# Two-layer block on one core: the second norm's sum taken from products of residual and update, and the next two weight units worked tile by tile

## The reference, cut to what matters

```python
h = _modulate(_rms_norm(x, g_pre_mix), sh1, sc1)
y = mixers(h @ w_in) @ w_out
x = x + g1 * _rms_norm(y, g_post_mix)
h = _modulate(_rms_norm(x, g_pre_ffn), sh2, sc2)
f = square(relu(h @ w_ff1)) @ w_ff2
x = x + g2 * _rms_norm(f, g_post_ffn)
```

## Time and profile before

| | |
|---|---|
| median of 3 runs | 1632.98 us (1628.01 to 1635.12) |
| the profiled execution | 1626.87 us, span 1624.9 us |
| PE busy | 1511.0 us, 93% |
| DVE busy | 969.8 us, 60% |
| ACT busy | 913.2 us, 56% |
| chain that ended last | PE 74%, DVE 13%, ACT 10% |
| PE's granted clock, mean | 0.97 of full speed |

### The profile page before, as it was taken

How to read it: one execution, slowest core, us unless ns; L and a number is a source line. 1 busy time by engine, 2 the same in 40 slices (tenths; PEclk the granted TensorE clock), 3 DMA queues, 4 the chain that set the end, 5 groups by cost and what they waited for, 6 DMA issues and landing times.

```text
span 1624.9 us, 25430 instructions
## 1 busy us (share of the span) xinstructions
PE 1511.0 (93%) x10123; PEld 1271.8 (78%) x10123; DVE 969.8 (60%) x1565; ACT 913.2 (56%) x1510; POOL 34.2 (2%) x74
## 2 busy tenths in 40 slices
PE   5999999989999999979988899998999999888887
PEld 3688456658888888838846799998999998887787
DVE  2464578473443434475768766667675766577555
ACT  5654676463232423465666654567786767477745
POOL 3000000000000000000000000000000000001100
PEclk9999999989999999999999999999999999999899
DMA  7731446333433233343316566564544444253232
GB/s 246 241 90 66 156 154 207 127 110 101 133 104 104 78 104 104 112 130 104 104 64 221 185 205 202 188 198 151 177 156 152 150 141 156 79 168 112 85 105 78
DMA packets 223638, 225.37 MB, mean 139 GB/s; under 512 B 8234, under 2 KB 222064, under 8 KB 223472
## 3 DMA queue, kind: packets, MB, share of 16 engines
q1 hardware_dynamic: 222816, 223.63, 42.8%
q0 software_dynamic: 704, 0.12, 0.0%
HBM read 222.68 MB, written 1.05 MB: 138 GB/s over the span
## 4 chain that ended last, share of the span: by engine, by line
PE 74%; DVE 13%; ACT 10%; issue 2%; DMA 1%; SPq 0%; POOL 0%; DVEq 0%; ACTq 0%; POOLq 0%
PE bank L1057 21%; PE bank L1059 21%; PE bank L1058 21%; ACT SH L1739 2%; PE bank L1105 2%; DVE wlo L2169 1%; ACT whi L1602 1%; PE bank L1265 1%; PE bank L1426 1%; DVE AP L2745 1%; PE bank L1454 1%; PE bank L1381 1%; ACT AP L2023 1%; DVE XT L2489 1%; DVE XN L2488 1%
## 5 line engine op out<-in xcount | busy, mean ns | idle before, releaser
L2169 DVE TENSOR_TENSOR wlo<-raw,whi 128x1024 fp32r<-128x1024 f32 (+2 forms) x322 | 387.8, 1208 | 254.1 <-ACT whi L1602 249.3
L1602 ACT ACTIVATE whi<-raw 128x1024 fp32r<-128x1024 f32 (+2 forms) x322 | 335.9, 1046 | 272.7 <-PE bank L1059 254.0
L1057 PE MATMUL bank<-HH,whi 128*128 128x512 f32 (+2 forms) x640 | 245.3, 383 | 18.7 <-DVE HL L2191 15.7
L1058 PE MATMUL bank<-HL,whi 128*128 128x512 f32 (+2 forms) x640 | 241.5, 377 | 0.0
L1059 PE MATMUL bank<-HH,wlo 128*128 128x512 f32 (+2 forms) x640 | 241.4, 377 | 0.0
L1057 PE MATMUL bank<-HA,whi 128*128 128x256 f32 x576 | 165.4, 287 | 13.6 <-DVE LA L2191 5.2
L1058 PE MATMUL bank<-LA,whi 128*128 128x256 f32 x576 | 162.5, 282 | 0.0
L1059 PE MATMUL bank<-HA,wlo 128*128 128x256 f32 x576 | 162.3, 282 | 0.0
L1057 PEld LDWEIGHTS bank<-HH,whi 128*128 128x128 f32 (+1 forms) x640 | 121.2, 189 | 47.4 <-issue 16.0
L1059 PEld LDWEIGHTS bank<-HH,wlo 128*128 128x128 f32 (+1 forms) x640 | 121.2, 189 | 22.9 <-issue 0.5
L1058 PEld LDWEIGHTS bank<-HL,whi 128*128 128x128 f32 (+1 forms) x640 | 121.4, 190 | 22.3 <-issue 0.9
(11 more groups left out here) (377 smaller groups left out, 3072.8 us busy)
## 6 DMA issues: line engine op xcount, KB each, us to landing
raw<-in_w_ff_dram SPq DMA_DIRECT2D x64, 1024.0 KB, 5.4
raw<-in_w_mod_dram SPq DMA_DIRECT2D x48, 1024.0 KB, 5.2
raw<-in_a_w_in_dram SPq DMA_DIRECT2D x40, 1024.0 KB, 5.1
raw<-in_w_in_dram SPq DMA_DIRECT2D x18, 1024.0 KB, 5.3
raw<-in_b_w_in_dram SPq DMA_DIRECT2D x9, 1024.0 KB, 5.3
raw<-in_w_out_dram SPq DMA_DIRECT2D x8, 1024.0 KB, 6.3
raw<-in_ple_w_gate_dram SPq DMA_DIRECT2D x8, 1024.0 KB, 5.2
raw<-in_a_w_out_dram SPq DMA_DIRECT2D x4, 1024.0 KB, 5.1
```

Source lines behind the costliest of these rows:

```text
L1057: nc.tensor.matmul(o, wh, xh, start=start, stop=False, skip_group_check=shared)
L1058: nc.tensor.matmul(o, wh, xl, start=False, stop=False, skip_group_check=shared)
L1602: f(whi[h % HALF_SLOTS][:, 0:n], raw[u.id % RAW_SLOTS][:, (h % 2) * n:(h % 2) * n + n], ACT.Copy)\
L2169: v.tensor_tensor(wlo[h % HALF_SLOTS][:, 0:n], raw[u.id % RAW_SLOTS][:, (h % 2) * n:(h % 2) * n + n], whi[h % HALF_SLOTS][:, 0:n].bitcast( ...
```

## The change

In the product phase ahead of a gap DVE keeps three running sums: `ACC` of y² as before, `ACCC` of (g·y)² and `ACCB` of x·g·y (with `PB` as scratch), where g is the gate with the norm's gain. Behind the last product PE sums them over the partitions by token, in columns (128x1 results, four per sum for 512 tokens), so that root, refinement and the polynomial for the new x² (`post_sums`) run on 128x4; PE spreads both factors over a bank each (`widen`, banks 3 and 4). `norm` then updates x and norms it in one pass. The sum of x² is carried on in `AC`, which `first_sum` fills once. ACT now makes `HH` and `H` of every tile. The two next units are worked tile by tile together, only two of the mods stay ahead of their end, and the third stands behind it.

```diff
     def gap_units(first, second):
-        u0 = without_step(*first)
-        made = [lone_mod(*fill.pop(0), 3 + n) for n in range(3)]
-        u1 = without_step(*second)
-        if len(fill) > 0:
-            made.append(lone_mod(*fill.pop(0), 6))
-        u0.halves, u1.halves = (3, 4), (3, 4)
+        u0, u1 = without_step(*first), without_step(*second)
+        made = [lone_mod(*fill.pop(0), bank) for bank in (5, 7, None)]
+        made[0].pick, made[1].pick = 3, 4
+        for u in (u0, u1):
+            u.halves, u.first_half_done = (3, 4), None
+        if not u0.packed:
+            u0.banks_from = 5
         return u0, u1, made
...
+    def gap_post(l, which, u1, made):
         steps.append(("post", l, which))
+        steps.append(("post_sums", l, which, u1))
+        steps.append(("mod_mm", made[0]))
+
+    def gap_norm(l, which, u0, u1, made):
+        gap_second[l, which] = u1
+        steps.append(("norm_sum", l, which))
+        steps.append(("mod_row", made[0]))
+        steps.append(("mod_mm", made[1]))
         steps.append(("norm", l, which, (0, KC)))
+        for k in range(KC):
+            steps.append(("one_k", u0, k))
+            steps.append(("one_k", u1, k))
+        steps.append(("mod_mm", made[2]))
+        steps.append(("mod_row", made[1]))
+        steps.append(("mod_row", made[2]))
+        steps.append(("unit", u0))
+        steps.append(("unit", u1))
+        for kind in ("mod_pick", "mod_col"):
+            for u in made:
+                steps.append((kind, u))
+        filler(1, (LAYERS, 0))
...
+        def widen(b, src, t):
+            for n, c in enumerate(chunks_of(t)):
+                ins = nc.tensor.matmul(b[:, n * P:(n + 1) * P], bc(src[:, c:c + 1], [P, P]), ident, start=True, stop=True)
+            return ins
...
+        def add_yy(l, which, m):
...
+                    ins = v.scalar_tensor_tensor(out=ACCC[:, ts_], in0=SQ[m % 2][:, ts_], scalar=fG2[:, m, 1 - s:2 - s], in1=ACCC[:, ts_],
+                                                 op0=ALU.mult, op1=ALU.add)
...
+        def add_xy(l, which, m, n=1):
...
+            ins = v.scalar_tensor_tensor(out=x, in0=y, scalar=8.0 / D, in1=x_old, op0=ALU.mult, op1=ALU.mult)
...
+                ins = v.tensor_tensor(acc, acc, x, ALU.add)
...
+        def post_sums(l, which):
...
+            chain(v.tensor_tensor(tmp, columns(banks[4], t, 4), r, ALU.mult))
+            chain(v.tensor_tensor(tmp, tmp, columns(banks[4], t, 0), ALU.add))
+            chain(v.tensor_tensor(tmp, tmp, r, ALU.mult))
+            v.tensor_tensor(acc, acc, tmp, ALU.add).then_inc(*s_poly.tick(("n",) + norm_after[l, which]))
...
+                if before is not None:
+                    dve.wait_ge(s_yg, s_yg.at(before + (b_ - 1,)))
+                    dve.wait_ge(s_wide, s_wide.at(("p",) + before))
+                    chain(v.tensor_tensor(x, YM[:, a_:b_, sl], bc(banks[3][:, 0:n_t].unsqueeze(1), wide_), ALU.mult))
+                    v.tensor_tensor(XT[:, a_:b_, sl], XT[:, a_:b_, sl], x, ALU.add)\
+                        .then_inc(*s_x_new.tick(*(before + (k,) for k in range(a_, b_))))
...
+                v.tensor_tensor(x, XT[:, a_:b_, sl], bc(root.unsqueeze(1), wide_), ALU.mult)\
```

More of the change, by code:

```diff
@@ L185, in build @@
     s_aa = signal("aa")
+    s_products = signal("products")
+    s_poly = signal("poly")
+    s_wide = signal("wide")
     s_ab = signal("ab")
@@ L531, in lone_mod, with w_in_units @@
         u = without_step(mod_units, l, m, m + 1)
[L532 removed]
+        u.alone, u.bank, u.pick = True, bank, bank
         return u
[L535 removed]
+    def w_in_units(l):
         t1 = ALL if l == 0 else X
         w, x = A["w_in"][l], ("h", l, "mix")
[L538 to L539 removed]
         fm(w, 0, COL_XBC + 512, 256, two, "win", (l, "bc"), x, [ALL, t1])
```

281 lines of the change are left out of this document (188 added, 93 removed).

## The result

| | before | after | ratio, 95% interval |
|---|---|---|---|
| median of the runs, us | 1630.74 (4 runs, 1628.01 to 1635.12) | 1656.85 (1652.89 to 1657.57) | 1.0153 [1.0122, 1.0184] |
| profiled execution, us | 1626.87 | 1652.89 | |
| span of the profile, us | 1624.9 | 1651.1 | |

The account below looks back on a forecast made before the run. PE was taken to bound the kernel, busy 1511.0 of 1624.9 us. Gaps of +0.9, -1.9 and +9.2, with +0.5 for the first sum, gave +8.7, say +9: 1636 profiled, 1642 as median; range 1623 to 1655.

Parts of the forecast that it names:

- A: The gap proper, from P to the next unit's first product: 15.4 us against 25.2 (first gap) and 25.0 (second).
- B: From the first product behind a gap to E, both units by tile: 25.45, 22.1 and 13.6 us.
- C: From E to the start of the unit after: a new hole, 10.3, 9.65 and 9.7 us in the three gaps.
- P: The end of the last product ahead of a gap, from which the prediction counts its times.
- tiny operations cost double: Upper bound on A: 18 us instead of 15.4, or +2.6 each gap, if tiny operations take twice as long.
- DVE's lag: Third gap: DVE's work of about 6.2 a unit against 5.5 adds up to about 3 us, last copy near 906.
- Column products: Within A, PE's four one-column products that turn a sum by token: 1.15 us taken, between 0.4 and 1.15.
- The second gap's length before: Old stretch from P to the third unit in the second gap, taken as 49.5 us.
- E: The end of both next units behind a gap: 40.85, 37.5 and 29.0 us behind P.
- Clock behind the gaps: Products behind each new hole run at a lowered clock: 1.3 us lost for each gap.
- Rival 1: The hole costs no clock and ACT's list runs closer: 7 us less, +2, 1635 us; chance 0.28.
- Rival 3: DVE fills up ahead of layer 0's gaps, copies and low halves late: +7 more, +16, 1649 us; chance 0.18.

Follow-up runs that it names:

- Units apart: Changed kernel with only the interleaving undone: the second unit runs whole behind the first, column norm kept; ratio 1.0086, median 1642.21 us.
- the half behind: Changed kernel with the second unit interleaved for its first four tiles only, its second half behind the first unit's end; ratio 1.0087, median 1644.26 us.
- the relus ahead of the half: Changed kernel with the high half that waits for the load made behind the second unit's relus; ratio 1.0153, median 1652.0 us.
- the clock held: Changed kernel plus three 128x512 products per gap, into a bank nobody reads, between the column products; ratio 1.0157, median 1651.7 us.
- the sums short: Changed kernel with part of both new sums left out (one column instead of all for the middle tiles); ratio 1.0102, median 1647.3 us.

## Why the prediction was wrong in size

It held that 23 us are won in A and B and more than that lost in C. The sign of the sum was right, the sum was not: for the three gaps with their clock and sums over ACC it gave +8.2, and it is 22.1 (+4.9, +5.8, +11.4) measured in the same way. Two steps failed: A's pieces were priced at the full clock, and the second gap's old length was misread. Point by point:

- **C: right, in place, cause and size.** Forecast 10.3, 9.65, 9.7; measured 10.85, 10.20, 10.18, together 1.6 more. The release by ACT's R at the pick, the copy in the second gap, and the high half that waits for the load (0.71) are in the rows above. Units apart, the half behind and the relus ahead of the half each took a part of it away, and together the last two left 1.7.
- **A: the step that failed.** "So A is 15.4" took every piece at durations of the full clock, though the earlier trace rows had 0.89 for the old gap and the earlier trace rows showed 0.50 behind 2.71 of idle. Measured 18.58, 17.70, 17.98, together 8.1 more. In layer 0 (3.2 and 2.3 of it) the clock is the cause. At the clock that I assumed the list was right: with the clock held, the last sum by token ended at P + 6.95, which is the prediction's own figure, DVE's third operation at P + 11.03 (forecast 11.25), A was 14.95. At half clock the sums end at P + 8.1, the third operation at P + 14.65. The bound of +2.6 a gap, "tiny operations cost double", was named and was too small for the first gap. In the third gap (2.6) it is first of all DVE's lag that was mis-sized: I had 6.2 of work a unit and the last copy ending 3.2 behind P, and it is 6.77 and 5.04, which is 1.8 of the 2.6. With the sums short A was 14.5 there.
- **Column products:** 1.15 for four was near: they take 0.94, at half clock 1.84. The Trainium skill, page "TensorE: Matmul & The Clock Gate", section "Back-to-back issue gap", would have given 0.1, or 0.4 at four passes, by its floor of about 25 ns (the same row has about 62 ns a product with hardware decode off). With the 25 ns the trace disagrees: it has 0.81 from one group of four to the next at a granted clock of 1.00, about 0.2 each.
- **The second gap's length before: misread**, 49.5 for 45.1, 4.4 us. With 45.1 the prediction's own sum for this gap is +2.5: the gain of 1.9 was never there. These 4.4 are also more than the 1.9 by which the median lies above the range.
- **B: right.** E less A is 25.55, 22.40, 13.39 against 25.45, 22.1, 13.6.
- **Clock behind the gaps:** 1.3 each forecast; 1.5, 1.5 and 0.7. The Trainium skill, page "TensorE: Matmul & The Clock Gate", section "Part 1: The HAM clock gate", has an idle array fall to half its clock. That agrees with the holes (0.50 from 330 to 335, behind 3.59 of idle; the mod at 1.94 behind 6.81). Rival 1, which had no loss, was wrong. What I was not prepared for is A, where PE's rows are without a hole and the clock is 0.54.
- **Rival 3**, DVE full ahead of layer 0's gaps, did not come: PE has no wait for DVE in the last 20 us ahead of them, and DVE's new sums end at P + 5.83 and 5.22 (forecast 5.8). Short sums make DVE 1.3 earlier than that in the first gap and take 2.3 and 1.1 off A, but the lateness was in the forecast. In layer 1, where the forecast had too little of it, they take 3.4 off.
- **Not in the sum:** the rest is +3.5, of which +5.2 is mostly the rhythm of a feed-forward in that one profile, and +1.4 the unit that now waits for a sum of mods (0.44 of DVE, and its picks); the others are the -2.4, +1.8 and -2.5 of the list above, which no run takes apart.

8.1 + 0.2 + 1.6 + 4.4 - 0.2 = 14.1, which is the miss in the gaps (13.9) to 0.2. With the 3.5, less the 0.5 that the sum had for the first sum, that is 16.9 of the 17 us. What stays open: why the clock falls while PE is busy with these products, why the three wide ones kept it up in the first gap of two kernels and not of two others, and what sets the rhythm.

## What to carry to other kernels

Before two pieces of work are run side by side, write down what covered the first one's tail, since here a list of relus, halves and a load of some 10 us had been free and became a hole. Price a stretch of small products at half clock unless the trace shows the same mix at full: here PE was busy for 10.00 of 10 us at 0.54. Three wide products that compute nothing made A shorter by 3.6 and 2.7 where PE was not waiting, and longer by 2.8 where it waited for DVE. And check the borders of the stretch before, each by its neighbours in the timeline; one row taken for another was 4.4 of the 17 us.
